# Two DRAM stores of attention tables move from ScalarE's instruction stream to SyncE's, between its weight loads

## The reference

```python
# first block: 8 heads, one 256 x 256 tile per head
logit_own = einsum('bhqd,bhkd->bhqk', qc, k_own) * scale + bias_t[:, rel_bucket(dist_own)]
logit_own = where(dist_own >= 0, logit_own, -inf)
# second block: 8 heads, windows of 4 grid rows x 16 columns
dc = col_idx - arange(GRID_W)[:, None] + (NA_COLS - 1)
s = einsum('bqhd,brqkhd->bhqrk', qr, kb) * scale + rpb[:, :, dc][:, dr]
```

## Time and profile before

| | |
|---|---|
| median of 3 runs | 3019.35 us (3014.46 to 3024.26) |
| the profiled execution | 3018.35 us |
| its span in the trace | 3016.6 us |
| PE busy | 2789.4 us (92%) |
| POOL busy | 2197.0 us (73%) |
| DVE, ACT busy | 1072.8 us (36%), 1210.7 us (40%) |
| moved by DMA | 589.75 MB |

### The profile page before, as it was taken

The page is one execution under the profiler, slowest core; times in us unless marked ns, Lnnn a source line. Parts: engine busy times, 40 slices in busy tenths (PEclk is TensorE's granted clock), DMA queues, the critical chain, the costliest instruction groups (busy, mean ns, idle before and its releaser), DMA issues.

```text
span 3016.6 us, 52183 instructions
## 1 busy us (share of the span) xinstructions
PE 2789.4 (92%) x21360; PEld 2711.5 (90%) x21360; DVE 1072.8 (36%) x1251; ACT 1210.7 (40%) x1439; POOL 2197.0 (73%) x889
## 2 busy tenths in 40 slices
PE   4799998977599999999999988999999999999997
PEld 3788998867599999999999977899999999999996
DVE  4554446646444544432235324461030000002233
ACT  3335343332253433334455344453353333334442
POOL 3577665545478889878888864586788888887894
PEclk7899899988799999999999999999999999999998
DMA  9897656555346666544545543363445555554552
GB/s 318 307 368 273 225 223 256 211 195 188 140 168 223 229 227 232 202 154 180 181 167 182 189 158 115 112 224 140 154 169 182 184 183 184 184 181 159 184 184 86
DMA packets 111618, 589.75 MB, mean 196 GB/s; under 512 B 23276, under 2 KB 25324, under 8 KB 54796
## 3 DMA queue, kind: packets, MB, share of 16 engines
q1 hardware_dynamic: 92592, 570.47, 52.0%
q10 hardware_dynamic: 18908, 17.58, 2.1%
HBM read 577.79 MB, written 10.21 MB: 195 GB/s over the span
## 4 chain that ended last, share of the span: by engine, by line
POOL 36%; issue 32%; PE 29%; DVE 1%; POOLq 1%; ACT 0%; DVEq 0%; ACTq 0%
POOL w_lo L454 36%; PE ps L1091 10%; PE ps L1095 10%; PE ps L1093 10%; POOLq L453 0%; PE ps L1176 0%; DVE res L2393 0%; POOLq L457 0%; ACT w_hi L474 0%; PE ps L1167 0%; DVE stage_v L1701 0%; DVE res L2064 0%; DVE ps L1685 0%; DVE ps L1682 0%; DVE rstd L1687 0%
## 5 line engine op out<-in xcount | busy, mean ns | idle before, releaser
L454 POOL TENSOR_TENSOR w_lo<-raw,w_hi 128x1024 fp32r<-128x1024 f32 x884 | 2196.6, 2499 | 785.8 <-ACT w_hi L474 783.0
L1091 PE MATMUL ps<-a_hi,w_hi 128*128 128x256 f32 x6512 | 1874.7, 288 | 117.2 <-POOL w_lo L454 43.5
L1093 PE MATMUL ps<-a_lo,w_hi 128*128 128x256 f32 x6512 | 1860.5, 286 | 0.0
L1095 PE MATMUL ps<-a_hi,w_lo 128*128 128x256 f32 x6512 | 1859.7, 286 | 0.0
L474 ACT CAST w_hi<-raw 128x1024 fp32r<-128x1024 f32 x884 | 918.3, 1047 | 1296.4 <-PE ps L1095 1135.4
L1091 PEld LDWEIGHTS ps<-a_hi,w_hi 128*128 128x128 f32 x6512 | 1270.2, 195 | 127.5 <-issue 52.7
L1093 PEld LDWEIGHTS ps<-a_lo,w_hi 128*128 128x128 f32 x6512 | 1269.7, 195 | 0.8
L1095 PEld LDWEIGHTS ps<-a_hi,w_lo 128*128 128x128 f32 x6512 | 1268.2, 195 | 0.0
L1808 DVE TENSOR_TENSOR a_lo<-arena,a_hi 128x1024 fp32r<-128x1024 f32 x44 | 107.6, 2448 | 348.4 <-ACT a_hi L816 348.4
L2356 DVE TENSOR_TENSOR work<-ps,rstd 128x512 f32<-128x512 f32 x22 | 15.2, 692 | 430.4 <-PE ps L1095 430.4
L1649 DVE SCALAR_TENSOR_TENSOR ps<-arena,small,ps 128x1024 f32<-128x1024 f32 x90 | 113.7, 1286 | 127.6 <-DMA arena<-ada 127.2
(11 more groups left out here) (181 smaller groups left out, 1266.5 us busy)
## 6 DMA issues: line engine op xcount, KB each, us to landing
raw<-stream SPq DMA_DIRECT2D x442, 1024.0 KB, 4.8
arena<-ada SPq DMA_DIRECT2D x192, 512.0 KB, 5.7
arena<-memT SPq DMA_DIRECT2D x4, 512.0 KB, 11.1
rel_rows<-arena ACTq DMA_DIRECT2D x1, 2048.0 KB
res<-xT SPq DMA_DIRECT2D x1, 2048.0 KB, 23.4
k_spill<-arena ACTq DMA_DIRECT2D x4, 512.0 KB, 8.7
v_spill<-arena ACTq DMA_DIRECT2D x4, 512.0 KB, 7.2
work<-rel_rows ACTq DMA_DIRECT2D x16, 128.0 KB, 2.2
```

The costliest lines, as they stand in the source:

```text
L454: pool.tensor_tensor(w_lo[:, h % SLOTS], raw_half(h), w_hi[:, h % SLOTS].bitcast(F32), ALU.subtract).then_inc(lo_ready, 1)
L1091: pe.matmul(o, w_hi[:, h % SLOTS, w], a_hi[:, c0 + k, :], start=first and k == 0 and f % 2 == 0, stop=False, skip_group_check=True)
L1093: pe.matmul(o, w_hi[:, h % SLOTS, w], a_lo[:, c0 + k, :], start=False, stop=False, skip_group_check=True)
L1095: mm = pe.matmul(o, w_lo[:, h % SLOTS, w], a_hi[:, c0 + k, :], start=False, stop=last and k == 1, skip_group_check=True)
```

## The change

The two stores are taken out of ACT's loop. SP issues the first (with its wait for `rel_row`) directly behind tile 8, and the second (with its wait for `rpb_in`) directly behind tile 20. The stores themselves are the same.

```diff
                 stream_tile(t)
                 if t == 6:
                     sp.dma_start(res[:, :, :], xT).then_inc(s_res, 16)
+                if t == 8:
+                    sp.wait_ge(rel_row, 1)
+                    sp.dma_start(rel_dram, tab_row.unsqueeze(1).broadcast_to([8, P, REL])).then_inc(scr_stored, 16)
+                if t == 20:
+                    sp.wait_ge(rpb_in, 16)
+                    sp.dma_start(rpb_dram, tab_rpb[:, 0:NA_W].unsqueeze(1).broadcast_to([56, GRID, NA_W]))\
+                      .then_inc(scr_stored, 16)
                 done = rows_by(max(2 * t - 9, -1))
                 until = min(160, done + (4 if done + 4 <= ADA_EARLY else 2))
                 for n in range(issued, until):
...
                     square2(3, memory[:, 12:16, :])
-                if h == 6:
-                    act.wait_ge(rel_row, 1)
-                    act.dma_start(rel_dram, tab_row.unsqueeze(1).broadcast_to([8, P, REL])).then_inc(scr_stored, 16)
-                    act.wait_ge(rpb_in, 16)
-                    act.dma_start(rpb_dram, tab_rpb[:, 0:NA_W].unsqueeze(1).broadcast_to([56, GRID, NA_W]))\
-                       .then_inc(scr_stored, 16)
                 if h in (18, 20, 22, 23):
```

## The result

| | before | changed |
|---|---|---|
| median | 3018.74 us (3011.10 to 3024.26, 8 runs) | 3031.88 us (3026.34 to 3037.08, 8 runs) |
| span of the profiled execution | 3016.6 us | 3035.3 us |

The change makes the kernel **slower: ratio 1.0046, 95% interval 1.0033 to 1.0059**, 13 us by the medians. The profiled execution of the changed kernel took 3037.08 us, the longest of its eight, so distances read from its trace are somewhat larger than those of the medians.

A forecast was written before the change was run, and what follows sets the result against it. The prediction took two PE pauses, 33 and 12 us, both from the table stores, as what the change could return. Term A, 6.5 us gained, and term B, 7 lost, gave −0.5 on 3018.35: 3018 us, range 2993 to 3034.

The forecast's parts named there:

- What bound the kernel: Before the change, PE's pauses of 33 us (from 47) and 12 us (from 96) both come from the table stores.
- part 1: Half 8: without the stores from 40 to 64 us, PE starts at 63 us instead of 80.4, 17.4 earlier.
- Part 2: Half 18: the first store holds q1 for 38 us, to 102; one 17 us pause replaces the second one.
- Part 3: Half 27: PE waits for row 31 and goes on at 145 us, where it was at 151.5 before.
- term A: Half 27: 6.5 us gained, being 108.5 less the end of the first store.
- Part 4: Second store behind tile 20: it costs q1 10 us; tiles bear that with 12 us to spare, row 63 doesn't.
- term B: Half 59: 7 us lost waiting for row 63, the store's 10 us less 2.8 to spare.
- part 5: ACT's waits for both stores, SP's added waits, and SP being held while the first store fills the rings cost nothing.
- The rule of the sum: Whole kernel: the gain is 47.5 us less the time for which the two stores together hold q1.
- the weights starve: First store takes 47.5 us in q1, second 13.3: 3032 us; decides once both take over 56.5 us; chance 0.24.
- The fast rival: First store at 104 ns per packet ends at 77 us, half 27 comes at 120: 2992 us; chance 0.30.

The follow-up runs named there:

- e2: The kernel before, with only the second store moved to SP behind tile 20, the first staying on ACT: 3015.75 us, ratio 0.9995.
- e3: The changed kernel, with the first table's 8 source rows four partitions apart (0, 4, ..., 28): 3000.75 us, ratio 0.9951 to the kernel before.
- e10: The changed kernel, with the first table's 8 source rows two partitions apart (0, 2, ..., 14): 3011.35 us, ratio 0.9976 to the kernel before.
- e8: The changed kernel, with second-table rows of 128 floats instead of 127 (512-byte packets): 3026.5 us, ratio 1.0037 to the kernel before.
- e5: As e3, but with the second store behind tile 33 instead of tile 20: 2989.68 us, ratio 0.9906 to the kernel before.
- e7: The changed kernel, but with the second store issued by ACT at h = 35, on q10: 3033.62 us, ratio 1.0045 to the kernel before.
- e9: As e7, but with the second store in two halves, at h = 35 and h = 41: 3021.85 us, ratio 1.0012 to the kernel before.
- e4: The kernel before, with the first table's 8 source rows four partitions apart (0, 4, ..., 28): 3004.18 us, ratio 0.9956.

## Why the prediction was wrong

**What bound the kernel, and part 1, held.** The two pauses and their causes are confirmed by e2. (One figure there is off without consequence: 21.43 MB in 54 us are 3.2 MB in 8 us, not 3.3.) Half 8 starts on PE at 64.5 us, where I had 63. Row 13 is used at 57.60, where I had 55.7; that is DVE's timeline in the changed kernel, its last row at the root against 79.90 in the earlier trace rows:

```profile
57.60 1.29 DVE L1650 SCALAR_TENSOR_TENSOR ps<-arena,small,ps 128x1024 f32<-128x1024 f32 x1 [7.56 <-DMA arena<-ada]
...
63.90 0.42 DVE L1688 SCALAR_TENSOR_TENSOR rstd<-ps,rstd 128x256 f32<-128x256 f32 x1
```

**Part 2, the first store in q1, held in its mechanism and was 4 us short in size.** The store started at 63.68, where I had 63.8, and ended at 105.75, where I had 102. One long pause replaced the second: PE was idle for 20.1 us ahead of half 18, which started at 115.7 instead of my 111. I had lowered the measured 41 us to 38, although gave 41 and the earlier trace rows 47.5, and only the first packets were faster.

**Part 3, term A, was mis-sized: predicted 6.5 us gained, measured 0.9 lost.** Of the 7.4 us, 4.7 are the late end of the wait: PE took up the sums ahead of half 27 at 149.67 where I had 145 (tile 9's cast came at 112.17, against 107.5). That was still 1.5 us earlier than the 151.22 of before. The rest, but for 0.3 us, is a term that I left out here, the slow restart behind a pause. In the changed kernel PE had been idle for 5.75 us when it went on, and in the kernel before it hadn't paused at all. Stretches as in the earlier trace rows, first the changed kernel, then the one before:

```profile
149.60:153.50 3.90, 3.83 (x10) 3.04 (x11) 0.04 (x1) 1.65 (x2) 3.12 (x2) 0.50 0.93 323
```

```profile
151.00:153.20 2.20, 2.20 (x16) 1.94 (x14) 0.05 (x1) 1.05 (x1) 1.90 (x2) 1.00 0.95 320
```

At a granted clock of 0.50, the lower of its two levels, instead of 1.00 the same eight matmuls took 3.75 us instead of 1.89, and by the end of half 27 the lead of 1.5 us had become the 0.9 us lost.

**Part 4, term B, is the step that failed most: predicted 7 us lost, measured 14.4.** Its rule, the store's length less the 2.8 us to spare at half 59, came close. Its size failed. The store was taken at 10 us and held q1 for 17.8; even the upper bound that I had written down, 13.3 us, was too low. From 176 to 188 us q1 moved 3158 packets, 3109 of them the store's: that is about the pace of the earlier trace rows. The last 475 took another 6 us, while a store of keys on q10 and the rows behind them shared the engines, and the bound left that tail out. The 10 us rested on all 16 engines joining at the packet time of the earlier trace rows, 38 ns; in q1 a packet took 55 ns on average. 17.8 less 2.8 gives 15.0 us. The same rule with the measured lengths gives 13.3, 13.7, 14.3 and 9.8 us for e2, e3, e10 and e8, and the losses measured from half 31 to half 63 are 11.7, 12.8, 12.9 and 8.7: each about 1 to 1.6 us less. DVE's timeline of the changed kernel shows the rows behind the store, then row 63:

```profile
195.82 2.48 DVE L1650 SCALAR_TENSOR_TENSOR ps<-arena,small,ps 128x1024 f32<-128x1024 f32 x2 [18.43 <-DMA arena<-ada]
...
256.18 1.29 DVE L1650 SCALAR_TENSOR_TENSOR ps<-arena,small,ps 128x1024 f32<-128x1024 f32 x1 [3.18 <-DMA arena<-ada]
```

Row 63 is used at 256.18 instead of 240.17, 16.0 us late, and PE waits 7.4 us for it at half 59. It goes on there at 258.56 where it was at 246.13, 12.4 us late, 0.9 of them from before; the rest of the 14.4 is the slow restart again, at a granted clock of 0.50 from 258.5 to 265.6 us. So the rows were late by a little less than the store's length, and the restart, which the rule leaves out, made up for that: that the rule comes so close is luck in part.

I also said that tiles bear the store, with 12 us to spare. By the same reckoning they bear 10 us, but not 17.8: the cast of half 42 waited 8.32 us for tile 21. Most of that ACT could spare. PE was idle for 2.1 us there and 0.9 us ahead of half 48, and up to half 58 the late tiles had cost 4.1 us; at half 59 another 10.1 came on top. What PE lost to the tiles it would probably have waited at half 59 anyway, since row 63 was late by itself (no run shows this directly): in e8 no tile made PE wait, and the loss still followed the store's length. SP was held here too. It stood at the issue of the next two rows until 186.03, and tile 21 was issued at 186.07, some 9 us behind its turn. But as part 5 has it, that cost nothing: the store ended at 194.04, and two rows and the tile landed behind it by 199.46, 5.4 us later, as fast as q1 moves them at its full rate (5.0 us).

**The rule of the sum**, that gain goes with the time for which the two stores hold q1, was right in kind. With 42.1 and 17.8 us it gives 12.4 us lost (59.9 less 47.5), against 13 by the medians and 15 at half 63 of the execution in which the lengths were measured; the slow restarts behind the pauses at halves 27 and 59 have no term in it. The rival that came true, "the weights starve", named the point of 56.5 us, and the measured 59.9 lies beyond it. It had the lower chance because I took values below both measured bounds, 38 and 10 us where 41 and 13.3 stood beside them. That its time was met within 1 us is luck in part: its 47.5 us for the first store were too many and its 13.3 for the second too few.

**The fast rival** (3 out of 10) was impossible as long as the rows lay in eight adjacent partitions. The bound of 104 ns from the earlier trace rows was the start of the store only. With the rows spread out (e3) such packets went on to the end of the store.

**The end.** From 474 us to the end the profiled execution loses another 3.4 us. Other kernels gain or lose about as much there, most of it between 540 and 740 us (e8 gains 3.7, e5 loses 3.6). I have no cause for it; the medians don't depend on one execution.

## What to carry to other kernels

A DMA that is slow by its source or by its packet size should not stand in the queue of a stream that has to be on time: count how long it holds the queue, to its last packet. On another queue it still holds that engine's next issue, and an engine that is held there stops its other work (e7), so place it where neither queue has anything due (e5), or split it (e9). First ask whether it must be slow at all: moving eight rows four partitions apart was worth 31 us in the queue of the weights and 13 on ScalarE's queue (e4), while the change itself cost 13.

## What the runs showed of the hardware

- A store from eight adjacent partitions went at 24 packets of 2 KB per us (50 GB/s) on either queue; from partitions two and four apart, in q1, at 51 and about 100 packets per us (105 and 205 GB/s).
- Issuing a DMA took under a microsecond, even one of 3584 packets, but the next issue of the same engine then took up to 20 us (19.65 and 20.31 us in the kernel before, 13.79 us in e7, where it came 15.8 us behind the store's own issue). In the change SP was held for 23.16 us over two issues.
- Packets of 508 bytes, with their store alone in q1, took 55 ns on average and the store 17.8 us; packets of 512 bytes took 33 ns and 12.6 us. Spread over 49 us on q10 (e9), packets of 508 bytes took 27 ns.
- Behind a pause of 5.75 us PE went on at a granted clock of 0.50, and eight matmuls took 3.75 us instead of 1.89.
